# Two hybrid layers ended in one code block each, and the third branch's gate products done earlier

## The reference

```python
for l in range(DEPTH):
    h = rmsnorm(x, norm1_g[l])
    x = x + hybrid_mixer(h, ...)
    h = rmsnorm(x, norm2_g[l])
    x = x + swiglu(h, w_ffn_gate[l], w_ffn_up[l], w_ffn_down[l])
return rmsnorm(x, final_norm_g)
```

## Time and profile before

| | us |
|---|---|
| median of 3 runs | 2412.97 (2411.13 to 2414.88) |
| the profiled execution | 2406.2 |
| its span, first to last instruction | 2404.4 |
| PE busy | 2098.0 (87%) |
| DVE busy | 1455.8 (61%) |
| ACT busy | 1037.7 (43%) |
| two hybrid layers, to PE's last sum of squares | 1330.2 |

### The profile page before, as it was taken

The page is one execution under the profiler, slowest core; times in us unless marked ns, Lnnn a source line. Parts: engine busy times, 40 slices in busy tenths (PEclk is TensorE's granted clock), DMA queues, the critical chain, the costliest instruction groups (busy, mean ns, idle before and its releaser), DMA issues. The chain is left out here.

```text
span 2404.4 us, 40251 instructions
## 1 busy us (share of the span) xinstructions
PE 2098.0 (87%) x16890; PEld 1989.7 (83%) x16890; DVE 1455.8 (61%) x2309; ACT 1037.7 (43%) x1444; POOL 0.2 (0%) x4
## 2 busy tenths in 40 slices
PE   4879798799869787987999677999979898899997
PEld 4878777699868787776999667999979876799997
DVE  3757555578658575555887564655548755555554
ACT  3643433344336433434443333444446544444443
POOL 0000000000000000000000000000000000000000
PEclk8989889899989897998999888999989997899999
DMA  4333423489843334233998322555534421445552
GB/s 171 123 106 106 125 75 109 140 286 314 302 145 115 97 115 132 71 114 131 317 328 292 121 81 77 178 184 180 182 113 150 149 80 44 140 149 179 182 183 97
DMA packets 101124, 371.73 MB, mean 155 GB/s; under 512 B 11344, under 2 KB 11600, under 8 KB 100560
## 3 DMA queue, kind: packets, MB, share of 16 engines
q1 hardware_dynamic: 99936, 363.90, 46.0%
q10 hardware_dynamic: 1008, 5.26, 0.6%
HBM read 368.07 MB, written 1.05 MB: 154 GB/s over the span
## 5 line engine op out<-in xcount | busy, mean ns | idle before, releaser
L292 DVE TENSOR_TENSOR low<-raw,high 128x1024 fp32r<-128x1024 f32 x594 | 725.9, 1223 | 566.4 <-ACT high L289 565.5
L355 PE MATMUL ps<-hh,high 128*128 128x256 f32 x3248 | 942.6, 290 | 87.7 <-PEq L585 59.4
L356 PE MATMUL ps<-hh,low 128*128 128x256 f32 x3248 | 925.9, 285 | 0.0
L357 PE MATMUL ps<-hl,high 128*128 128x256 f32 x3248 | 924.5, 285 | 0.0
L289 ACT CAST high<-raw 128x1024 fp32r<-128x1024 f32 x594 | 620.7, 1047 | 641.5 <-PE ps L357 604.2
L355 PEld LDWEIGHTS ps<-hh,high 128*128 128x128 f32 x3248 | 638.0, 196 | 108.1 <-issue 99.6
L356 PEld LDWEIGHTS ps<-hh,low 128*128 128x128 f32 x3248 | 636.1, 196 | 0.6 <-issue 0.5
L357 PEld LDWEIGHTS ps<-hl,high 128*128 128x128 f32 x3248 | 635.8, 196 | 0.0
L356 PE MATMUL ps<-hidden_high_half,low 128*128 128x256 f32 x512 | 143.0, 279 | 0.0
L355 PE MATMUL ps<-hidden_high_half,high 128*128 128x256 f32 x512 | 142.9, 279 | 0.0
L357 PE MATMUL ps<-hidden_low_half,high 128*128 128x256 f32 x512 | 142.6, 279 | 0.0
(11 more groups left out here) (386 smaller groups left out, 2735.8 us busy)
## 6 DMA issues: line engine op xcount, KB each, us to landing
raw<-in_stream SPq DMA_DIRECT2D x594, 512.0 KB, 3.7
ada_rows<-in_ada SPq DMA_DIRECT2D x96, 512.0 KB, 5.0
bias<-in_bias ACTq DMA_DIRECT2D x1, 1536.0 KB, 7.3
xT<-in_xT ACTq DMA_DIRECT2D x1, 1024.0 KB, 3.9
c_act<-in_c SPq DMA_DIRECT2D x2, 512.0 KB, 4.4
out<-xT SPq DMA_DIRECT2D x1, 1024.0 KB, 3.9
par<-in_par ACTq DMA_DIRECT2D x1, 910.0 KB, 12.9
hybrid_const<-in_const ACTq DMA_DIRECT2D x1, 800.0 KB, 9.8
```

The costliest lines, as they stand in the source:

```text
L292: return dve.tensor_tensor(self.low[:, slot, :], self.raw[:, slot, :], self.high[:, slot, :].bitcast(F32), ALU.subtract)
L355: pe.matmul(out, sh, mh, start=start, stop=False, **more)
L356: pe.matmul(out, sl, mh, start=False, stop=False, **more)
L357: return pe.matmul(out, sh, ml, start=False, stop=stop, **more)
```

## The change

**The end of a layer is one block.** `feed_forward` holds the last four units of the mixture, the output product, the second norm, the hidden and the down product, and in layer 0 also the first norm and the first four pairs of projections of layer 1. `Entry` does a norm without a stop: x times gain (without 1/rms) is split as soon as a pair of tiles is ready, the first four pairs of the next product run on it, and 1/rms is multiplied onto their results; meanwhile the sum of squares (one-column matmuls), root, reciprocal and a spread over partitions are made, and the fully normed h is built for the fifth pair on. The mixture's halves and the hidden values are waited for k pair by k pair in the next product's first tile (`ready`).

**The start** is one block as well: ACT loads x, both layers' parameters and what is needed first, the four units are split in turn with x. `const1` and `par3` are loaded later in that block, the second stack's parameters (`par2`) in the last norm's block.

**The gate products of the third branch** (turns 8 to 11, eight units) are moved: four units into `compress` behind the window products, four into `compressed_probabilities` behind turn 3; the stream is reordered the same way (`MIX_ORDER`). Their tanh values are kept in tiles no longer used. In `feed_forward` the four branch units remain. In `compressed_probabilities` DVE now does its mixture work before it waits for the transposed probabilities.

**The ada rows** begin two iterations later: 24 in the hidden product (iterations 2 to 9 of 11), 24 in the down product, where the last unit and the eleventh have two.

```diff
+TURNS = N_BR * KD // 2
+AHEAD = TURNS - KD // 2
+
+
+def whole_turns(turns):
+    return [3 * n + c for n in turns for c in range(3)]
+
+
+def gate_turns(turns):
+    return [3 * n + c for n in turns for c in range(2)]
+
+
+MIX_ORDER = (whole_turns(range(3)) + gate_turns((AHEAD, AHEAD + 1)) + whole_turns((3,)) +
+             gate_turns((AHEAD + 2, AHEAD + 3)) + whole_turns(range(4, AHEAD)) + [3 * n + 2 for n in range(AHEAD, TURNS)])
...
+            def rows(self, i):
+                return IN_SWIGLU + (i + 1) * (ADA - IN_SWIGLU) // self.n
+
+            def unit(self, dve, i):
+                self.w.vector(dve, i)
+                if self.mods is not None:
+                    self.mods.vector(dve, self.rows(i))
...
+            def weigh(self, dve, n):
+                c = n % (KD // 2)
+                if n >= 2:
+                    dve.wait_ge(*self.at(split_x, KD, n - 1))
+                for m in range(2):
+                    k, to = 2 * c + m, self.staged[:, n % 2, m, :]
+                    if n < KD // 2:
+                        ins = dve.tensor_scalar(to, xT[:, k, :], self.gain[:, k:k + 1], None, ALU.mult)
+                    else:
+                        ins = dve.scalar_tensor_tensor(to, xT[:, k, :], self.gain[:, k:k + 1], self.row, ALU.mult, ALU.mult)
+                tell(ins, weighed)
...
+            def late(self, pe, c):
+                pe.wait_ge(*self.at(split_x, KD, KD // 2 + c + 1))
+
+            def add_sums(self, pe, c):
+                pe.wait_ge(*self.at(squares, KD // 2, c + 1))
+                for k in (2 * c, 2 * c + 1):
+                    for t in range(TT):
+                        ins = pe.matmul(ps[:, 4 + t, 0:1], sq[:, k, t * P:(t + 1) * P], ones[:, 0:1], start=(k == 0),
+                                        stop=(k == KD - 1), skip_group_check=True)
+                if c == KD // 2 - 1:
+                    tell(ins, summed)
+
+            def spread(self, pe):
+                pe.wait_ge(*self.at(rstd_column, 1, 1))
+                for t in range(TT):
+                    ins = pe.matmul(ps[:, 6, t * P:(t + 1) * P], first_halves[:, 2, t:t + 1].broadcast_to([P, P]), ident,
+                                    start=True, stop=True)
...
+            def tensor(self, pe, res, product):
+
+                for j in range(KD // 2 if res is not None else 0):
+                    res.tensor(pe, j)
+                    if j:
+                        self.add_sums(pe, j - 1)
+                u = (self.uh, self.ul)
+                product(pe, 0, u, 0, self.early)
+                if res is None:
+                    pe.wait_ge(loaded, 16 * 2)
+                    for c in range(KD // 2 - 1):
+                        self.add_sums(pe, c)
+                self.add_sums(pe, KD // 2 - 1)
+                product(pe, 0, u, 1, None)
+                self.spread(pe)
+                for j in range(1, EARLY):
+                    product(pe, j, u, None, None)
+
+            def scalar(self, act, res, product):
+
+                if res is None:
+                    first_parameters(act)
+                    act.wait_ge(x_loaded, 16 * (1 + DEPTH))
+                act.activation(first_halves[:, 3, :], xT[:, 0, 0:TT], ACT.Square)
+                for j in range(KD // 2):
+                    if res is not None:
+                        res.scalar(act, j)
+                    else:
+                        first_round(act, j)
+                    self.round(act, j)
+                    square_tiles(act, j)
+                self.deviation(act)
+                c = KD // 2
+                self.round(act, c)
+                product(act, 0)
+                self.round(act, c + 1)
+                product(act, 1)
+                if res is None:
+                    bounds_exponentials(act)
+                    late_parameters(act)
+                self.round(act, c + 2)
+                self.round(act, c + 3)
+                product(act, 2)
+                product(act, 3)
+
+            def vector(self, dve, res, product):
+
+                for j in range(KD // 2):
+                    if res is not None:
+                        units = list(res.prod.units_of(j))
+                        for i in units[:-1]:
+                            res.unit(dve, i)
+                        res.add(dve, j)
+                        res.prod.after_read(dve, j)
+                    else:
+                        first_split(dve, j)
+                        if j == 0:
+                            dve.wait_ge(x_loaded, 16 * (1 + DEPTH))
+                    self.weigh(dve, j)
+                    if res is not None:
+                        res.unit(dve, units[-1])
+                    self.split(dve, j)
+                if res is None:
+                    bounds_differences(dve)
+                if res is not None and res.mods is not None:
+                    res.mods.finish(dve)
+                self.column(dve)
+                self.take_row(dve)
+                c = KD // 2
+                self.weigh(dve, c)
+                product(dve, 0)
+                self.weigh(dve, c + 1)
+                self.split(dve, c)
+                product(dve, 1)
+                if res is None:
+                    bounds_logarithms(dve)
+                self.weigh(dve, c + 2)
+                self.split(dve, c + 1)
+                self.weigh(dve, c + 3)
+                self.split(dve, c + 2)
+                product(dve, 2)
+                self.split(dve, c + 3)
+                product(dve, 3)
...
-            mine = mix.take(turns)
+            taken = mix.take(turns)
+            mine, last = taken[:6], taken[6:]
...
                                 ins.then_inc(ring.unit_done.sem, 1)
+                    for p in last:
+                        mix.tensor(pe, p)
                     pe.wait_ge(to_pe2.sem, to_pe2.base + 2)
-                    pe.matmul(ps[:, 6, 0:2 * NCMP], P1("w2_k"), hid[:, 0, :], start=True, stop=True)
...
                     tell(dve.tensor_tensor(pc, pc, over_keys(cstat[:, 3, :], 32), ALU.mult), prob_ready)
+                    for p in mine:
+                        mix.vector(dve, p)
                     dve.wait_ge(pt_done.sem, pt_done.base + 1)
                     dve.tensor_copy(W[:, 2, 0:BANK], ps[:, 6, :])
-                    for p in mine:
-                        mix.vector(dve, p)
...
+            def rows(i, u):
+                return min(max(3 * (i - 2) + min(u, 2) + 1, 0), IN_SWIGLU)
...
                 def _(sp):
+                    mix.sync(sp)
+                    out.sync(sp)
                     for i in range(w.n):
-                        mods.sync(sp, min(i // 4 * 3 + min(i % 4, 2), IN_SWIGLU))
                         w.sync(sp, [i])
+                        mods.sync(sp, rows(i // 4, i % 4))
+                    down.sync(sp)
+                    if proj is not None:
+                        proj.sync(sp)
 
                 @block.tensor
...
+                    for p in mine:
+                        mix.tensor(pe, p)
+                    entry.tensor(pe, out, lambda pe, j, x, only, ready: prod.tensor(pe, x, j, only, ready))
+                    for j in range(EARLY, KF):
+                        prod.tensor(pe, h, j, None, entry.late if j == EARLY else None)
+                    if proj is not None:
+                        entry2.tensor(pe, down, lambda pe, j, x, only, ready:
+                                      proj.early_tensor(pe, projected[j], x, only, ready))
...
+                    for i, p in enumerate(mine):
+                        mix.vector(dve, p)
+                        if i:
+                            split_mix(dve, i - 1)
+                    split_mix(dve, turns - 1)
+
+                    def early(dve, j):
+                        i = j // 2
+                        b3 = buf(i).rearrange("p (m t) -> p m t", m=2)
+                        acc3 = prod.wait(dve, j).rearrange("p (m t) -> p m t", m=2)
+                        if j % 2 == 0:
+                            dve.tensor_tensor(b3, acc3, row, ALU.mult).then_inc(prod.read(j), 1)
+                            for u in range(2):
+                                w.vector(dve, 4 * i + u)
+                            dve.wait_ge(to_dve2.sem, to_dve2.base + i + 1)
+                            done(dve.tensor_tensor(b3, b3, row, ALU.mult))
+                        else:
+                            dve.tensor_tensor(b3, b3, acc3, ALU.mult).then_inc(prod.read(j), 1)
+                            for u in range(2, 4):
+                                w.vector(dve, 4 * i + u)
+                            low_part(dve, i)
+
+                    def low_part(dve, i):
+                        dve.wait_ge(to_dve.sem, to_dve.base + i + 1)
+                        tell(dve.tensor_tensor(flat(fl[:, 2 * i:2 * i + 2, :]), buf(i),
+                                               flat(fh[:, 2 * i:2 * i + 2, :]).bitcast(F32), ALU.subtract), to_act)
...
+            rope(mix, 3)
```

(44 more changed lines are left out.)

498 lines of the change are left out of this document (282 added, 216 removed).

## The result

The changed kernel takes 2396.07 us (median of 4, 2393.46 to 2398.19) against 2413.93 (median of 4, 2411.13 to 2418.71): ratio 0.9923, 95% interval 0.9903 to 0.9944. It is faster, by 18 us and not by 38. The profiled execution took 2398.19 us, span 2396.4, granted clock 0.922 (0.914 before).

A forecast was written before the change was run, and what follows sets the result against it. PE was taken as the bound, draining at block ends, with the pair of ada-row buffers a second bound in the down products. Terms -9-8-16.4-11.5-5-2+13.5 = -38.4 gave 2375 us from 2413, range 2346 to 2403.

The forecast's parts named there:

- The parts behind are unchanged.: Everything behind the final norm, the second stack included: forecast to change by 0 us.
- Start: Kernel's beginning as one block: next block's first matmul at 57.4 instead of 66.34 us, -9 (-4 to -14).
- Gate products and mixture: Eight gate units moved from the mixture into compression and probabilities: -4.0 us per layer, -8.0 in all (each +1 to -8).
- Output product and hidden product: Stretch from output product through hidden product, waits at its end gone: -19.7 us in layer 0, -13.2 in layer 1.
- Down products: 24 ada rows at 3.19 us outlast PE's work: -2 us in layer 0 with next entry, +13.5 in layer 1.
- Rival 1: Ada rows don't hold up the down products, PE sets both ends: -65 us, 2348; chance 0.14.
- Final norm: Last norm also loads par2, 0.88 MB: hidden under the norm's 7 us, or +6; taken as 0.
- Rival 2: Clock stays down through new thin places at entries and mixtures, five at 3 us: -22 us, 2391; chance 0.16.
- Rival 3: Ada rows choke in the down products, landing after 7.5 us instead of 5.1: +18 us, 2431; chance 0.07.
- Rival 4: DVE's early work holds PE at every entry, norms cost as before: entries +25, 2400; chance 0.05.

The follow-up runs named there:

- the two pads: Changed kernel with 224 bytes left free ahead of xT and 32 behind lb, so xT, hh, hl and sq stand at their old places within 256: 2374.41 us, ratio 0.9846.
- the four buffers: Changed kernel with four buffers for the ada rows instead of two, nothing else: 2369.13 us, ratio 0.9846 to the kernel before.
- 27 in the other: Kernel before the change with 32 bytes left free ahead of xT and 32 more behind lb: 2436.72 us, ratio 1.0114.

## Why the prediction was wrong, by its own steps

- **The step that failed: "The parts behind are unchanged."** I counted instructions, and by that it was true. But the change moved tiles, hh and hl from 192 to 224 bytes of distance, and there every matmul starts 3 to 4 ns later (118.3 ns against 114.4 in the second stack). The term that I put at nothing measured +18.3 us, and the two pads take 17.5 of it back. In the hybrid layers they take another 7.0 (1329.98 to 1322.98). That is 24.5 us in the profiled executions and 18.6, give or take 7, by the ratios with and without the pads (0.0077 of 2413). Either is the size of the miss of 20.
- **The closeness that is left is in part luck.** With the pads the total is 37 us under the kernel before by the ratios, 32.5 in the profiled executions; the forecast was 38. Errors of both signs stand in it, below, and one gain that I had not foreseen: the feed-forward halves, moved from 96 bytes to 192, went from 120.0 ns to 116.6 and 115.9 in the down products, some 4 us of PE for 1056 matmuls, while the early pairs at 64 and 128 run slower than hh did. How much of either reached the total no run shows, since the ada rows set those stretches.
- **Start, -9 forecast, -0.5 measured.** The row of 1/rms came at 40.7 instead of 34.5. The first product matmul came at 15.58, not 12 to 13: ACT waits for the layer parameters until 11.22, whose DMAs landed 8.8 us after issue, and x took 6.5 instead of the earlier trace rows's 3.9, all crowded with the weights. The sums were 32 records of 0.213 us in one batch, 6.8, where I counted 16, 4: each float32 matmul stands as two records. And the whole second unit ran with starts 0.213 us apart, against 0.118 behind the spread (the profile's clock column reads 1.00 there and does not show it): 5.3 us, where my 34.5 left about 4. From the row on it took 25.2 us against 23.
- **Gate products and mixture, -4 a layer forecast, -3.0 and -2.2 measured (22.1 - 25.1 and 22.4 - 24.6), by a wrong mechanism.** What the units add in front was near (22.1 and 22.4 against 23). But with the units put back the layer is 2.3 us faster: the move costs, and the mixture without them saves 22, not 26. I had booked to them the 3 us that the one-block end saves at the mixture. DVE's earlier mixture work in the probabilities block, which I put at 1.6, gave 2.3.
- **Output product and hidden product: right**, -19.0 and -14.7 against -19.7 and -13.2, at a slower pitch than the forecast's. The hole behind the last pair is 0.4 us where 1.3 was worked out, the waits just before and in the ninth unit come to 2.2 where 3.0 was, and no hole stands at the hidden product's end. Nor does a drain show at the table loads: Silu's at 472.12 starts 0.02 us after the rounding before it, and Silu itself at 473.41, 0.01 us behind it.
- **Down products: mechanism right, size near.** The pace is 3.24 and 3.12 us against 3.19. In layer 0 the next block begins 113.0 us after the down product's start, 108.5 forecast. The last split was on time (81.6 against 82.5); then sums and second unit took 7.7 instead of some 6, at a granted clock of 0.55 behind the hole of 12.2 us, and from the spread on it was 23.6 instead of 20.4. In layer 1 it cost 9.0, not 13.5: DVE was done 78.6 us after the start instead of 81, and the kernel before had taken 69.3, not 67.5. Rival 1 (the rows don't hold it up) is excluded by that pace and priced by the four buffers: 13.7 and 10.2 us, where it said 14 and 13.5. The formula of the Trainium skill (DMA: Bandwidth & Descriptors, Anatomy of one DMA), which gave an estimated pace of 2.8, does not agree with the trace: the rows land 5.1 and 5.0 us (median, layers 0 and 1) after issue, where it gave an estimated 4.4. The page fits it for DMAs issued from GpSimd; these are issued from SP.
- **Final norm, nothing forecast: right.** It loads par2 beside, 4.6 us, hidden: from DVE's last step of layer 1 to the second stack's first matmul it is 26.1 us, 26.4 before.
- **Rival 2 (clock)** named 2391, near what was measured, by a wrong mechanism: the granted clock rose from 0.914 to 0.922 over the span, and it is 0.99 in both stretches with the output product and its entry, where the rival wanted it low. It was low at layer 0's end, behind the rows' hole. Its own sum was slightly off: five places at 3 us are 15, not 16. **Rival 3** did not come. **Rival 4** came in part, at layer 0's end alone (the 12.2 us), and by the rows, not by the early work. Had I stopped at the total, rival 2 would have looked confirmed.

## What to carry to other kernels

When a tile is added or removed, work out where the others come to lie: for these products the places of a few tiles were worth 18.6 us in one kernel and 27 in the other, with no instruction changed. Compare first the stretches that a change does not touch; a difference there is a cause of its own, and it must come off before the steps are judged. A transfer of 5.1 us behind two buffers with 1.2 us of work each gives 3.2 us a row, whatever the engines could do; count buffers against the landing time before moving rows into a shorter stretch.

## What the runs showed of the hardware that I had not expected

The start-to-start distance of float32r matmuls of 128 x 256 at 2.4 GHz depends on the distance in SBUF between weights and moving tile within 256 bytes: with TensorE alone 113.6 ns at 192, 117.4 to 118.6 at 32, 64, 128, 160 and 224, 119.8 to 119.9 at 0 and 96, to a tenth or so the same in three turns. It was measured in steps of 32 bytes, for this shape and order of products only; in full kernels tiles at 192 also run at 118 ns, and why the distance matters stays open.
